# Inverse levels of a chunked scan: which half of the partitions holds a transposed inverse, and where the next head's keys are computed

## The chip, the cores and the metric

One NeuronCore of one Trainium2 chip runs the whole program. The time is device microseconds from launch to end; the median of the runs shown counts. PE is TensorE, PEld its weight loads, DVE VectorE, ACT ScalarE, POOL GpSimd, SP SyncE.

## The reference

Two layers of a hybrid trunk (an RWKV-7 mixer with a Fourier mixer, then a convolution mixer with gating), each followed by an expert-choice mixture of experts, for 512 sample tokens and 128 prompt tokens at width 1024. The change lies in the RWKV-7 mixer, 12 heads of 64 columns, both directions of time. Its recurrence, cut to what matters:

```python
def step(S, inp):
    r_t, w_t, k_t, v_t, kk_t, a_t = inp
    s_kk = jnp.einsum('zbhvk,zbhk->zbhv', S, kk_t)
    S = (S * w_t[..., None, :] - s_kk[..., None] * (kk_t * a_t)[..., None, :]
         + v_t[..., :, None] * k_t[..., None, :])
    return S, jnp.einsum('zbhvk,zbhk->zbhv', S, r_t)
```

All arithmetic is f32.

## The kernel before, in words

The recurrence is computed in tiles of 128 tokens. Within a tile the tokens' corrections of one another form a triangular system, and its 128x128 matrix has to be inverted, once for each of 5 tiles (the **groups** g below, NT = 5), 2 directions (z) and 2 heads (hh), since two heads make up the 128 partitions of one pass; there are six passes ("heads" in the code, `for i in range(HP - 1): heads(True)` and then `heads(False)`; "head" here means such a pass). The first five have `following` set: while one is scanned, the next one's projections are computed between its steps. The last one has no next.

A 128x128 triangle is treated as two 64x64 triangles and a corner. Each 64x64 triangle is inverted by doubling: in six **levels** blocks of 1, 2, 4, ... 32 are joined. `xx` holds, for each group, direction and head, the inverse (slot 1, `inv`) and its transpose (slot 0, `invT`) of both 64x64 blocks, one block in each half of the partitions. A block's inverse lies in the half in which the block itself lies in `mat`; its transpose lies in the other half. A level of one group goes round four engines' steps:

- `correct` (L1023), TensorE: 16 products of 64x64 from `yw` and `invT` into two PSUM banks, (4, 5) or (6, 7), by turns of the group's number. The first inner line (L1029) reads and writes the same half, the second (L1033) crosses to the other half. `first_correct` (L1011) does the same for the first level, where the products are mere copies and transposes.
- VectorE (L1646 to L1658): two predicated copies, one a direction, take the masked part of those banks into `xx` (`copy_predicated`, L1652); each of them says `x_new`.
- `middle` (L1036), TensorE: 8 products of 64x64 (L1043) of `mat`'s block and `inv`, all crossing, into bank 2 or 3.
- ScalarE (L1341 to L1344): one copy of 128x256 into `yw` says `yw_copied`.

The five groups run staggered, in an order written out by hand on TensorE (the listing below): first level; then a loop of four **turns**, each with the corrections of groups 0 to 4 and the middles of groups 3, 4, 0, 1, 2; then the last level, where `corner_middle` and `corner` make the corner blocks. A turn of the loop is a level of all five groups. `take(name, n)` waits for n signals.

Between the groups lie `keys` (L1064): matmuls of 128x128 by 128 columns that project one of the next head's five tiles of 128 tokens onto its keys, 8 for a tile, into PSUM banks 0 and 1. In the first level they stand in three places (3, 3 and 2 of the 8), in each turn in three places (2, 2 and 4).

VectorE does eight pieces of the previous head's output (`tail`, L1607: four reciprocals, scaling, shift, gate, bonus) in between, one after every third group from the start of the levels. After the last level, where it signals `x_new` only once its copies have ended (`done`), it copies the transposed inverses into `mat` (L1659 to L1661, ten copies), and TensorE waits for them (`blocks_copied`) and for the corners (`corner_copied`) before the scan (L1167).

TensorE's matrix is used in quarters here: with 64 rows read and 64 partitions written, four products can be in flight, each in its own quarter. An f32 product leaves two matmul records in the trace.

## Time and profile before

| | us |
|---|---|
| median of three runs | 2407.01 (2406.4 to 2408.57) |
| profiled execution, its own time | 2403.96 |
| its span, first to last instruction | 2402.1 |
| TensorE busy | 2259.6 (94%) |
| VectorE busy | 934.6 (39%) |
| ScalarE busy | 397.0 (17%) |
| mean granted TensorE clock | 0.982 of 2.4 GHz |

The busy time of TensorE is that of pipelined matmuls, so a busy TensorE need not be at its peak; shares over the whole span mix stages with different limits. The six heads lie between about 200 and 850 us of the span. The levels of head 0 run from 222.40 to 268.52, those of the last head from 798.67 to about 839.

### The profile page before, as it was taken

What the parts mean: (1) busy time and instruction counts of PE and PEld (TensorE: products, weight loads), DVE (VectorE), ACT (ScalarE), POOL (GpSimd) and SP (SyncE); (2) the same over time, 40 slices, a digit from 0 to 9 for tenths busy, and PEclk for the clock granted to TensorE, in tenths of its full rate; (3) what the DMA queues carried; (4) which work ended last, traced back from release to release, by engine and by line L of the source; (5) the groups of instructions that cost most, each with busy time, mean ns of one, the idle gap of its engine ahead of it and who ended that gap; (6) DMA issues with size and microseconds to landing.
All of it is one profiled execution on the core that took longest, in us unless ns stands there. A gap on an engine that the chain in (4) does not pass through costs nothing. (4 is left out here: it accounts for less than half of the span.)

```text
span 2402.1 us, 56100 instructions
## 1 busy us (share of the span) xinstructions
PE 2259.6 (94%) x23412; PEld 1292.7 (54%) x23412; DVE 934.6 (39%) x1965; ACT 397.0 (17%) x685; POOL 167.0 (7%) x162
## 2 busy tenths in 40 slices
PE   5998999999999889899999999889998999999997
PEld 2446777777686765544444444545555444444444
DVE  1357666676767621311111111479513111111113
ACT  2022323232323301100000000211312000000001
POOL 1001010100001000000000000000000000000000
PEclk8998999999999999999999999999999999999999
DMA  9981010101010025799999999602036999999995
GB/s 362 376 316 48 2 33 2 32 3 32 3 32 13 10 82 231 260 379 396 392 395 396 391 396 391 206 1 70 1 140 252 395 396 394 393 397 392 392 392 172
DMA packets 181670, 538.56 MB, mean 224 GB/s; under 512 B 12545, under 2 KB 54145, under 8 KB 181410
## 3 DMA queue, kind: packets, MB, share of 16 engines
q1 hardware_dynamic: 175202, 515.16, 55.8%
q0 software_dynamic: 6336, 21.63, 3.8%
q8 instruction: 84, 1.38, 0.2%
q14 instruction: 48, 0.39, 0.1%
HBM read 510.81 MB, written 25.95 MB: 223 GB/s over the span
## 5 line engine op out<-in xcount | busy, mean ns | idle before, releaser
L2115 PE MATMUL ps<-raw,xs 128*64 128x512 f32 x3072 | 670.9, 594 | 4.9 <-PEq L2109 4.9
L2115 PEld LDWEIGHTS ps<-raw,xs 128*64 128x64 f32 x3072 | 217.2, 137 | 429.4 <-issue 428.1
L2127 PE MATMUL ps<-raw,xs 128*32 128x256 f32 x6144 | 342.4, 380 | 2.2 <-PEq L2109 2.2
L2127 PEld LDWEIGHTS ps<-raw,xs 128*32 128x32 f32 x6144 | 195.2, 110 | 133.0 <-issue 9.7
L2306 DVE SCALAR_TENSOR_TENSOR h<-h,ps 128x768 f32<-128x768 f32 x32 | 30.5, 954 | 460.9 <-DVEq L2305 460.9
L1652 DVE COPY_PREDICATED wk<-m,ps 128x128 f32<-128x128 uint8 x360 | 101.8, 352 | 123.1 <-DVEq L1648 122.7
L2433 PE MATMUL ps<-h,raw 128*128 128x512 f32 (+1 forms) x448 | 124.0, 438 | 7.2 <-PEq L2424 7.2
L2234 ACT ACTIVATE h<-ps 128x768 f32<-128x768 f32 x32 | 25.9, 811 | 591.1 <-ACTq L2233 591.1
L899 PE MATMUL ps<-h,wk 128*128 128x512 f32 (+1 forms) x416 | 121.4, 438 | 1.5 <-PEq L1224 1.3
L1029 PE MATMUL ps<-wk 64*64 64x64 f32 x2400 | 102.2, 223 | 5.5 <-PEq L1005 5.2
L2433 PEld LDWEIGHTS ps<-h,raw 128*128 128x128 f32 x448 | 68.7, 193 | 62.0 <-issue 62.0
L1043 PE MATMUL ps<-wk 64*64 64x64 f32 x2400 | 97.0, 218 | 1.0 <-PEq L1005 0.8
L1033 PE MATMUL ps<-wk 64*64 64x64 f32 x2160 | 97.8, 222 | 0.1
L2694 DVE SCALAR_TENSOR_TENSOR wk<-wk 128x670 f32<-128x670 f32 x116 | 96.4, 914 | 0.4 <-DVEq L2688 0.4
L1344 ACT ACTIVATE wk<-ps 128x256 f32<-128x256 f32 (+1 forms) x180 | 65.8, 366 | 184.1 <-ACTq L1343 184.0
L2090 POOL DMA_INDIRECT ysum<-rows,idx x30 | 43.1, 1437 | 753.7 <-POOLq L2088 744.7
L899 PEld LDWEIGHTS ps<-h,wk 128*128 128x128 f32 x416 | 66.2, 191 | 53.5 <-issue 53.5
L1029 PEld LDWEIGHTS ps<-wk 64*64 64x64 f32 x2400 | 82.8, 133 | 14.2 <-issue 6.9
L1043 PEld LDWEIGHTS ps<-wk 64*64 64x64 f32 x2400 | 85.3, 135 | 1.6 <-issue 1.6
L2295 DVE TENSOR_TENSOR xs<-ps,mod 128x512 f32<-128x512 f32 x68 | 30.2, 486 | 140.3 <-DVEq L2292 140.3
L1641 DVE TENSOR_TENSOR wk<-ps,tables 128x512 f32<-128x512 f32 x120 | 74.6, 684 | 15.4 <-DVEq L1640 15.4
L1033 PEld LDWEIGHTS ps<-wk 64*64 64x64 f32 x2160 | 80.1, 134 | 0.2 <-issue 0.2
(333 smaller groups left out, 2673.5 us busy)
## 6 DMA issues: line engine op xcount, KB each, us to landing
raw<-in_moe_w_gate SPq DMA_DIRECT2D x64, 2048.0 KB, 17.5
raw<-in_moe_w_up SPq DMA_DIRECT2D x64, 2048.0 KB, 18.0
raw<-in_moe_w_down SPq DMA_DIRECT2D x64, 2048.0 KB, 18.3
wk<-in_mod_w SPq DMA_DIRECT2D x24, 2048.0 KB, 11.0
wk<-in_ev_w_in SPq DMA_DIRECT2D x18, 512.0 KB, 5.3
raw<-in_od_w_in SPq DMA_DIRECT2D x4, 2048.0 KB, 17.7
hrow<-rows SPq DMA_DIRECT2D x10, 512.0 KB, 3.0
ysum<-low SPq DMA_DIRECT2D x10, 512.0 KB, 8.9
```

The source lines that it names most:

```text
L899: last = pe.matmul(pair(q)[:, a:b], win[:, c, s], h[:, c, a:b], start=c == 0, stop=c == KC - 1)
L1029: pe.matmul(ps[lo:hi, zb, slotT(z, hh):slotT(z, hh) + HD], yw[lo:hi, g, z, hh], invT(g, z, hh, lo, hi), start=True, stop=True)
L1033: last = pe.matmul(ps[to:te, zb + 1, slotN(z, hh):slotN(z, hh) + HD], invT(g, z, hh, lo, hi), yw[lo:hi, g, z, hh], start=True, stop=True)
L1043: last = pe.matmul(ps[to:te, mbank(g), at:at + HD], mat[lo:hi, g, z, hh, 0, lo:hi], inv(g, z, hh, lo, hi), start=True, stop=True)
L1344: act.activation(yw[:, g].rearrange("p z h n -> p (z h n)")[:, 0:w], ps[:, mbank(g), 0:w], ACT.Copy).then_inc(sem("yw_copied"), 1)
L1641: dve.tensor_tensor(mat[:, tt, z, hh].rearrange("p k n -> p (k n)"), ps[:, 4 + (n + 2) % 4], tri[:, z], ALU.mult).then_inc(sem("mat_read"), 1)
L1652: dve.copy_predicated(changed(xx[:, g, z].rearrange("p k h n -> p k (h n)"), z, lev), changed(bcast(lv[:, lev, z], 1, 2), z, lev), changed ...
L2090: pool.indirect_dma_start(t["ysum"][:, :], bass.IndirectOffsetOnAxis(idx[:, e:e + 1], 0), ys[:, ee], None, compute_op=ALU.add).then_inc(se ...
L2115: last = pe.matmul(ps[to:to + CAPS, bank_of(kind, ee)], XS[ee][:, c, 0:CAPS], raw[:, slot(l, 2 * m + c // 4), c % 4, 8 * to:8 * to + 512], ...
L2127: last = pe.matmul(ps[to:to + 32, bank_of(kind, ee) + 1, 0:256], XS[ee][:, c, CAPS:], raw[:, slot(l, 2 * m + c // 4), c % 4, 8 * to:8 * to ...
L2433: last = pe.matmul(place(q)[:, a:b], win[m // 4][:, c, m % 4 * P:(m % 4 + 1) * P], h[:, c, a:b], start=c == 0, stop=c == KC - 1)
L2694: dve.scalar_tensor_tensor(to, src, cw[:, c, k:k + 1], to, ALU.mult, ALU.add).then_inc(sem("tap"), 1)
```

## The change

One of the four combinations of direction and head, (0, 0), keeps its transposed inverse in the half of its own block. For it, `correct`'s second product and `middle`'s product no longer cross; the product of `middle` goes to a place of its own in bank 1, the same one for all groups, so `middle` waits for its last copy. `correct` does the four combinations in another order, (0, 0) last. ScalarE copies a middle in two pieces (64 and 192 columns), each with a signal. VectorE copies a group in three pieces instead of two (four in the first level, with a wait), each with a signal. In the last level it copies the near transposed inverse over to the other half, where `corner` reads it from `yw`. The block copies into `mat` become six, each over all groups. All eight keys of a tile stand in one place: in the first level ahead of group 2's first correction, in a turn at its end. The tail pieces follow a level's fifth group: two behind each of the first three levels, then one and one. In the diff's core, `corrections` and `correction` are VectorE's copies:

```diff
+            TAIL = ((0, 1), (2, 3), (4, 5), (6,), (7,), ())
...
                         def correct(g, both=True):
...
+                            for z, hh in ((0, 1), (1, 0), (1, 1), (0, 0)):
+                                near = z == 0 and hh == 0
+                                for lo, hi in HALF:
+                                    pe.matmul(ps[lo:hi, zb, slotT(z, hh):slotT(z, hh) + HD], yw[lo:hi, g, z, hh], invT(g, z, hh, lo, hi), start=True, stop=True)
+                                for k, (lo, hi) in enumerate(HALF):
+                                    to, te = HALF[1 - k]
+                                    if near and (both or k == z):
+                                        last = pe.matmul(ps[lo:hi, zb, 4 * HD:5 * HD], invT(g, z, hh, lo, hi), yw[lo:hi, g, z, hh], start=True, stop=True)
+                                    if not near and (both or k != z):
+                                        pe.matmul(ps[to:te, zb + 1, slotN(z, hh):slotN(z, hh) + HD], invT(g, z, hh, lo, hi), yw[lo:hi, g, z, hh], start=True, stop=True)
                             last.then_inc(sem("z_ready"), 1)
...
+                        def middle(g, far_free, near_free):
+
+                            if far_free:
+                                take("yw_copied", far_free)
+                            for z, hh in ((0, 1), (1, 0), (1, 1)):
+                                for k, (lo, hi) in enumerate(HALF):
+                                    to, te = HALF[1 - k]
+                                    at = (z * 2 + hh) * HD
+                                    pe.matmul(ps[to:te, mbank(g), at:at + HD], mat[lo:hi, g, z, hh, 0, lo:hi], inv(g, z, hh, lo, hi), start=True, stop=True)
+                            if near_free:
+                                take("yw_copied", near_free)
+                            for lo, hi in HALF:
+                                last = pe.matmul(ps[lo:hi, 1, P:P + HD], mat[lo:hi, g, 0, 0, 0, lo:hi], inv(g, 0, 0, lo, hi), start=True, stop=True)
                             last.then_inc(sem("yw_ready"), 1)
...
                         with pe.Fori(0, LEVELS - 2) as lev:
+                            take("x_new", 6)
                             correct(0)
+                            middle(3, 1, 1)
                             correct(1)
+                            middle(4, 1, 1)
+                            take("x_new", 3)
+                            correct(2)
+                            middle(0, 3, 0)
+                            take("x_new", 3)
+                            correct(3)
+                            middle(1, 0, 1)
+                            take("x_new", 3)
+                            correct(4)
+                            middle(2, 1, 1)
                             if following:
+                                keys(lev)
...
+                            if u < NZ - NT:
+                                act.activation(product[:, 0:HD], ps[:, 1, P:P + HD], ACT.Copy).then_inc(sem("yw_copied"), 1)
+                                act.activation(product[:, HD:4 * HD], ps[:, mbank(g), HD:4 * HD], ACT.Copy).then_inc(sem("yw_copied"), 1)
...
+                            if lev == 0:
+                                correction(g, lev, 0, 0, 1, ps[:, zbank(g) + 1, 4 * HD:5 * HD]).then_inc(dve_done, 1)
+                                correction(g, lev, 0, 1, 2, ps[:, zbank(g), HD:2 * HD]).then_inc(new, 1)
+                                correction(g, lev, 0, 2, 4, ps[:, zbank(g) + 1, 0:2 * HD]).then_inc(new, 1)
+                                done()
+                                corrections(g, lev, 1).then_inc(new, 1)
+                            else:
+                                corrections(g, lev, 0).then_inc(new, 1)
+                                correction(g, lev, 1, 0, 3, ps[:, zbank(g), 2 * HD:5 * HD]).then_inc(new, 1)
+                                correction(g, lev, 1, 3, 4, ps[:, zbank(g) + 1, 3 * HD:4 * HD]).then_inc(new, 1)
                             if q >= NZ - NT:
-                                done(2)
-                                dve.sem_inc(sem("x_new"), 2)
-                            if q % 3 == 2 and q < 3 * KC:
-                                tail(q // 3, i)
+                                done(3)
+                                dve.tensor_copy(yw[0:HD, g, 1, 0], xx[HD:P, g, 0, 0, 0]).then_inc(dve_done, 1)
+                                done()
+                                dve.sem_inc(sem("x_new"), 3)
+                            if g == NT - 1:
+                                for k in TAIL[lev]:
+                                    tail(k, i)
                         for lo, hi in ((0, HD), (HD, P)):
-                            for g in range(NT):
-                                dve.tensor_copy(mat[lo:hi, g, :, :, 0, lo:hi], xx[P - hi:P - lo, g, :, 0]).then_inc(dve_done, 1)
-                        done(2 * NT)
+                            dve.tensor_copy(mat[lo:hi, :, 0, 0, 0, lo:hi], xx[lo:hi, :, 0, 0, 0]).then_inc(dve_done, 1)
+                            dve.tensor_copy(mat[lo:hi, :, 0, 1, 0, lo:hi], xx[P - hi:P - lo, :, 0, 0, 1]).then_inc(dve_done, 1)
+                            dve.tensor_copy(mat[lo:hi, :, 1, :, 0, lo:hi], xx[P - hi:P - lo, :, 1, 0]).then_inc(dve_done, 1)
+                        done(6)
```

## Rows read from the trace of the kernel before

In a windows row the stretch and its length come first, then busy us and instruction counts of PE, PEld, DVE, ACT and POOL.

**Rows 1.** Page, the 40 equal slices: busy tenths of the 16 DMA engines.
```profile
DMA  9981010101010025799999999602036999999995
```

**Rows 2.** Windows of head 0 by stage, then granted clock, DMA share, GB/s.
```profile
222.40:229.86 7.46, 6.75 (x165) 6.02 (x165) 4.41 (x11) 1.75 (x4) 0.00 (x0) 1.00 0.01 2
229.86:237.43 7.57, 7.57 (x257) 7.01 (x257) 5.50 (x12) 1.92 (x5) 0.00 (x0) 1.00 0.02 4
...
244.94:252.45 7.51, 7.51 (x257) 6.95 (x256) 3.74 (x12) 1.92 (x5) 0.00 (x0) 1.00 0.00 0
...
259.97:268.52 8.55, 7.69 (x241) 6.61 (x241) 5.09 (x24) 4.42 (x13) 1.56 (x3) 1.00 0.01 3
```

**Rows 3.** The same view, the four turns of the last head.
```profile
804.75:830.15 25.40, 20.81 (x963) 19.83 (x964) 17.17 (x49) 7.66 (x20) 0.00 (x0) 1.00 0.01 2
```

**Rows 4.** Timeline of TensorE in a turn: start us, us, line, tiles, count.
```profile
245.05 0.23 PE L1029 MATMUL ps<-wk 64*64 64x64 f32 x2
...
245.40 0.23 PE L1029 MATMUL ps<-wk 64*64 64x64 f32 x2
...
245.47 0.46 PE L1043 MATMUL ps<-wk 64*64 64x64 f32 x10
245.72 0.27 PE L1029 MATMUL ps<-wk 64*64 64x64 f32 x2
```

**Rows 5.** Timeline of TensorE around two key places of that turn.
```profile
243.85 1.16 PE L1068 MATMUL ps<-h,wk 128*128 x8
244.94 0.27 PE L1029 MATMUL ps<-wk 64*64 64x64 f32 x2
...
246.97 0.71 PE L1068 MATMUL ps<-h,wk 128*128 x4
247.61 0.27 PE L1029 MATMUL ps<-wk 64*64 64x64 f32 x2
```

**Rows 6.** Timeline of VectorE, head 0: a small instruction, copies, tail pieces.
```profile
204.78 0.26 DVE L1626 TENSOR_SCALAR wk<-wk 64x64 f32<-64x64 f32 x1
...
223.36 1.29 DVE L1652 COPY_PREDICATED wk<-m,ps 128x128 f32<-128x128 uint8 x4 [4.33 <-DVEq L1648]
...
231.26 1.11 DVE L1579 RECIPROCAL x<-x 128x160 f32<-128x160 f32 x1
...
245.82 0.49 DVE L1652 COPY_PREDICATED wk<-m,ps 128x128 f32<-128x128 uint8 x2 [0.96 <-DVEq L1648]
...
248.89 0.61 DVE L1589 TENSOR_SCALAR x<-x,wk 128x640 f32<-128x640 f32 x1
...
250.72 0.92 DVE L1652 COPY_PREDICATED wk<-m,ps 128x128 f32<-128x128 uint8 x4 [0.26 <-DVEq L1648]
```

**Rows 7.** Timeline of VectorE, head 0: last level, block copies, a dependent instruction.
```profile
260.82 0.50 DVE L1652 COPY_PREDICATED wk<-m,ps 128x128 f32<-128x128 uint8 x2 [1.67 <-DVEq L1648]
...
264.36 0.50 DVE L1652 COPY_PREDICATED wk<-m,ps 128x128 f32<-128x128 uint8 x2 [0.35 <-DVEq L1648]
265.10 2.24 DVE L1661 COPY wk<-wk 64x256 f32<-64x256 f32 x10 [0.24 <-DVEq L1454]
...
269.43 0.88 DVE L1491 SCALAR_TENSOR_TENSOR x<-x,wk 128x640 f32<-128x640 f32 x1 [0.16 <-DVEq L1454]
```

**Rows 8.** Timeline of ScalarE, head 0: copies of 256 and 128 columns.
```profile
246.24 0.38 ACT L1344 ACTIVATE wk<-ps 128x256 f32<-128x256 f32 x1 [1.80 <-ACTq L1343]
...
263.24 0.28 ACT L1344 ACTIVATE wk<-ps 128x128 f32<-128x128 f32 x1 [0.35 <-ACTq L1343]
```

**Rows 9.** Timelines of VectorE and TensorE, last head, end of first level.
```profile
803.32 1.29 DVE L1652 COPY_PREDICATED wk<-m,ps 128x128 f32<-128x128 uint8 x4 [0.26 <-DVEq L1648]
...
804.75 0.27 PE L1029 MATMUL ps<-wk 64*64 64x64 f32 x2 [1.35 <-PEq L1005]
```

**Rows 10.** Timeline of TensorE, head 0: fifth group's corner product, and the scan's start.
```profile
265.31 0.45 PE L1051 MATMUL ps<-wk 64*64 64x64 f32 x8
...
268.52 0.74 PE L1167 MATMUL ps<-wk 128*128 128x64 f32 x5 [0.48 <-PEq L1156]
```

More of the change, by code:

```diff
@@ L1025, in correct @@
                             zb = zbank(g)
-                            for z in range(2):
-                                for hh in range(2):
-                                    for lo, hi in HALF:
-                                        pe.matmul(ps[lo:hi, zb, slotT(z, hh):slotT(z, hh) + HD], yw[lo:hi, g, z, hh], invT(g, z, hh, lo, hi), start=True, stop=True)
-                                    for k, (lo, hi) in enumerate(HALF):
-                                        if both or k != z:
-                                            to, te = HALF[1 - k]
-                                            last = pe.matmul(ps[to:te, zb + 1, slotN(z, hh):slotN(z, hh) + HD], invT(g, z, hh, lo, hi), yw[lo:hi, g, z, hh], start=True, stop=True)
@@ L1034, in correct @@
-                            last.then_inc(sem("z_ready"), 1)
-                        def middle(g):
-                            for z in range(2):
-                                for hh in range(2):
-                                    for k, (lo, hi) in enumerate(HALF):
-                                        to, te = HALF[1 - k]
-                                        at = (z * 2 + hh) * HD
-                                        last = pe.matmul(ps[to:te, mbank(g), at:at + HD], mat[lo:hi, g, z, hh, 0, lo:hi], inv(g, z, hh, lo, hi), start=True, stop=True)
+                            for z, hh in ((0, 1), (1, 0), (1, 1), (0, 0)):
[8 more added lines that the diff above has]
+                                        pe.matmul(ps[to:te, zb + 1, slotN(z, hh):slotN(z, hh) + HD], invT(g, z, hh, lo, hi), yw[lo:hi, g, z, hh], start=True, stop=True)
@@ L1059, in corner, with keys @@
                                     at = (g - first) * P + hh * HD
-                                    last = pe.matmul(ps[lo:hi, bank, at:at + HD], yw[lo:hi, g, 0, hh], invT(g, z, hh, lo, hi), start=True, stop=True)
+                                    block = yw[lo:hi, g, 1, 0] if z == 0 and hh == 0 else invT(g, z, hh, lo, hi)
+                                    last = pe.matmul(ps[lo:hi, bank, at:at + HD], yw[lo:hi, g, 0, hh], block, start=True, stop=True)
                             if g == end - 1:
                                 last.then_inc(sem("corner_ready"), 1)
-                        def keys(tt, chunks):
+                        def keys(tt):
                             at = slice(tt * P, tt * P + P) if isinstance(tt, int) else bass.ds(tt * P, P)
-                            for c in chunks:
+                            for c in range(KC):
                                 last = pe.matmul(pair(0)[:, at], win[:, c, K], h[:, c, at], start=c == 0, stop=c == KC - 1)
-                            if chunks[-1] == KC - 1:
-                                last.then_inc(sem("keys_ready"), 1)
+                            last.then_inc(sem("keys_ready"), 1)
                         first_correct(0)
@@ L1080, in heads @@
                             take_weights()
-                            keys(ST, (0, 1, 2))
-                        take("x_new", 2)
+                            keys(ST)
+                        take("x_new", 3)
+                        first_correct(2)
+                        middle(0, 0, 0)
+                        take("x_new", 3)
                         first_correct(3)
-                        middle(1)
-                        if following:
-                            keys(ST, (3, 4, 5))
```

75 lines of the change are left out of this document (28 added, 47 removed).

## The prediction

> **What bounds the kernel now.** I read the page's slices first. From the middle on, the 16 DMA engines are busy nine tenths of the time with the experts' weights; in the slices of the even layer's heads (about 200 to 850 us) they are nearly idle [rows 1]. Nothing there waits for memory, and the experts' loads start when that layer ends, so a microsecond won or lost in a head should arrive at the end. The change touches one stretch of each of the six heads, the inverse levels. The stage windows cut head 0 by its turns: 7.46 us for the first level, about 7.5 for each of the four turns of the loop (two shown), 8.55 for the last level and the corners; TensorE is busy through every turn, at full clock (1.00, 2.4 GHz), VectorE for half to three quarters, ScalarE for a quarter [rows 2]. So the turns hang on TensorE. The last head has no next head whose keys it could compute: its turns take 25.40 us together, or 6.35 each, and TensorE has gaps [rows 3]. It shows what the turns wait for once the keys are gone.
>
> Inside a turn the array works in quarters: half of the rows read, half of the partitions written. A matmul leaves two records, and a quarter starts one every 0.059 us (six steps from 245.05 to 245.40, a seventh to the middle's first at 245.47 [rows 4]). Of a group's 24 products 8 stay in their own half and 16 cross, so each straight quarter has 8 records and each crossing quarter 16: 16 x 0.059 = 0.94 us a group, 4.72 for five. The keys make up the rest of 7.51: 2.8 us, though 16 records alone are 1.8: eight hold TensorE from 243.85 to 244.94, four from 246.97 to 247.61 [rows 5], so a record is (1.09 - 0.64) / 4 = 0.1125 us and a place costs (2.8 - 1.8) / 3 = 0.33 besides; 16 records in one place are 2.13.
>
> **What is taken away.** Two of three key places go: 0.67 us a turn. One product in four now stays straight, so each quarter gets 12 records: 12 x 0.059 = 0.71 us a group in place of 0.94. That needs straight records of the next part to run beside crossing ones of the part before. [Rows 4] show it: at 245.72 L1029 starts while six of the sixteen L1043 that stand ahead of it in the program are still to come. The near products share one place in PSUM, so each waits for ScalarE's copy of the one before: 0.06 (its second record), 0.36 (L1043's eighth start at 245.88 to ScalarE's at 246.24 [rows 4, 8]), 0.23 (the copy: 256 columns are 0.38, 128 are 0.28 [rows 8]) and 0.14 for the way back (804.61 to 804.75 [rows 9]): 0.79 us. Behind that wait in TensorE's queue stands the next correction. I take 0.71 a group where it does not bind and 0.78 where it does.
>
> **What is added.** VectorE's two copies a group become three (four, with a wait, in the first level). The columns stay the same; an instruction is added. From the third level on, two copies are 0.49 and four 0.92, so one every 0.21 [rows 6]: 0.13 for 128 columns and 0.08 besides; three then take 0.58. In the first two levels (four in 1.29, [rows 6]) the columns cost double: three 0.74, the first level's four 0.88. ScalarE copies twice a group; the far copy ends 0.46 after the near one starts, against 0.38. The tail pieces of the previous head's output, until now one after every third group, come in pairs after a level's fifth group: 1.11 and a pause, 2.64 a pair; the scale-and-shift pair, with 1.83 from its shift to the next copy, is 2.8 [rows 6]. In the last level each group gets a copy of 64 columns between two waits. Nothing is loaded, and no DMA queue moves.
>
> **The turn worked out**, from its first correction. The group's ten straight records bring VectorE's first copy at 0.95 (today 0.88 with eight: 244.94 to 245.82 [rows 5, 6]). With 0.58 and 0.14, the third correction may start at 1.67; TensorE would be there at 1.42. Group 4's near product starts last at 1.36, its far copy ends at 1.36 + 0.36 + 0.46 = 2.18, and the first group's middle, which today has keys ahead of it, starts at 2.32 and not at 2.08. The fourth correction follows at 2.62, the fifth at 3.40, the keys at 4.18, their end (2.13) at 6.3: against 7.51, 1.2 us won. Turn by turn:
> - First level: 1.2 for two groups, keys 2.13, then group 2 waits 0.95 + 0.88 + 0.14 for its copies, and so does group 4: 7.3 against 7.46. The keys' gain is lost because nothing now covers the last wait; the last head shows that wait open today, 1.35 us [rows 9].
> - Turn 1: the tail pair, begun when group 4's copies end 0.14 before the turn, holds VectorE until 2.50, the third correction waits until 3.38, the fifth for slow copies until 5.21; with 0.78 and 2.13, 8.1 against 7.57.
> - Turns 2 and 3: the pair runs 1.4 us into the turn, the third correction comes at 2.13, which costs 0.2: 6.55 each. Turn 4: 6.3.
>
> The turns make 27.5 against 30.1: 2.6 won, with the first level 2.8.
>
> **The last level** gives most of it back. There the groups follow one another on VectorE: copies begin at 260.82 and, four groups on, at 264.36, with a pause of 0.35 behind each group's wait [rows 7]. To each come 0.08 (third copy), a wait for the own result (0.16 at 269.43 [rows 7]) and a 64-column copy: a copy of 128 alone is 0.28 (0.49 - 0.21), half its columns less 0.22, and a 64x64 instruction is 0.26 [rows 6]; I take 0.22, by the price of the columns. That is 0.46 a group, 2.3 for five, less 0.15 where VectorE now waits for TensorE: 2.1 us. Behind the added waits stand the next group's copies, and TensorE's corrections and corner products wait for their release. The end cannot hide it: the fifth group's corner product (265.31 [rows 10]) waits for exactly this release. Bounds: 1.0, if copy and pause overlap; 2.6, if all of it counts. The block copies become six in place of ten, some 0.3 shorter; today they end at 267.34 [rows 7], and TensorE goes on at 268.52 [rows 10], so I count nothing.
>
> **Sum.** A head with keys: -2.8 + 2.1 = -0.7, five of them -3.4. The last head has no keys to merge: turn 1 at 7.0, then 6.4 and 6.55 with tail pairs uncovered, and 5.1, 25.1 against 25.40 [rows 3]; with 2.1 from the last level, +1.8. Together -1.6 us. The profiled execution took 2403.96 us, 3.05 below the median of the runs; it would take 2402.4, and the median 2407.01 becomes **2405.5**.
>
> **The rivals.**
> - *Slower: the quarters don't mix (0.12).* If straight records wait until the crossing ones ahead of them have started, a group's parts line up: ten records, then six, then the near pair, 1.0 us where today's is 0.94. Turns 2 to 4 stay near 7.5, turn 1 takes 8.5, the last level's 2.1 is left: +3 a head, +18 in all, 2425. With the step at 0.85 it would be some +5, 2412; from there the change loses. [Rows 4] speak against it. The Trainium skill (TensorE: Matmul & The Clock Gate, Part 3, What overlaps and what doesn't) says that matmuls are strictly first in, first out in start and end; by that rule this rival would be the forecast, and the start at 245.72 contradicts it here.
> - *Slower: a predicated copy has one price whatever its width (0.12).* No row shows one of 96 or 32 columns. At 0.21 (0.28 early) each, VectorE takes 0.71 a group and 1.01 early, the first level's chain grows by 0.8, turn 1 by 0.6, turns 2 and 3 by 0.4 each, the last level by 0.7: +2.9 a head over the forecast, +15, 2421; at half of it 2413. It decides from about 0.65 a group. The other instructions of [rows 6] get shorter with width, which speaks against it.
> - *Faster: the last level costs only its lower bound (0.30).* If the added copy starts inside the pause that is there anyway, the price is 1.0, a head wins 1.8, the last loses 0.7: -8, 2399. For it: a group's 0.35 already holds one wait. Against it: the copy reads what the three before it wrote, so its own wait must come first.
> - *The forecast (0.46)*, 2402 to 2411: gain in the turns and price in the last level cancel.
>
> A measurement of this kernel tells about 0.2%, 4.8 us, from no change. Faster by more is the third rival, 0.30; slower by more the first two, 0.24; between them 0.46. The range runs from 2397 (the third rival with a turn a little better than worked out) to 2414 (half of either slower rival).
>
> **What would show it.** In the changed profile: one key place a turn of 16 records in about 2.1 us; L1029's successor and the middle starting within each other, 0.71 to 0.78 us between corrections; turns of 8.1, 6.55, 6.55 and 6.3; in turn 1 an idle TensorE for 1.5 us or more while VectorE does two reciprocals in a row; in the last level VectorE's groups 1.3 us apart in place of 0.85, and the corners about 2 us later. Wrong would be: groups 0.9 us or more apart (first rival), copies of 32 columns as long as those of 128 (second), last-level groups under 1.1 us apart (third).

## The result, and the profile after

The changed kernel takes 2417.78 us (median of five runs, 2416.72 to 2418.23); the kernel before took 2406.40 beside it. The ratio is 1.0048, 95% interval 1.0036 to 1.0059: **slower by 11.4 us**, outside the forecast range. The profiled execution took 2418.23 us with a span of 2416.3, that of before 2403.96 with 2402.1.

Where the 14.2 us between the two spans lie follows from two moments of each head, its first correction and the start of its scan, read from TensorE's timeline:

| us | before | after |
|---|---|---|
| levels of heads 0 to 5 | 46.10, 46.56, 46.51, 46.27, 46.38, 40.19 | 46.01, 49.83, 49.11, 47.83, 47.67, 41.71 |
| their sum | 272.0 | 282.2 |
| between the heads' levels | 344.4 | 344.7 |
| behind the last head's levels | 1563.2 | 1568.0 |
| ahead of the first | 222.4 | 221.5 |

The levels lose 10.1 us, and all of it in heads 1 to 4 and the last; head 0, by which the forecast was worked out, gains 0.1. The part behind the levels grows by 4.8. The change does not touch it, and it lies anywhere between 1563 and 1572 us in the fourteen kernels profiled here, one execution each, with the kernel before at the low end; what moves it is not shown.

The windows of after, by stage, columns as in [rows 2]: head 0's first level, turns 1, 2 and 4 and last level; turn 1 of heads 1 to 4; the last head's four turns.

```profile
221.46:228.62 7.16, 6.16 (x185) 5.75 (x185) 3.95 (x21) 1.93 (x7) 0.00 (x0) 1.00 0.01 2
228.62:236.54 7.92, 6.56 (x257) 6.18 (x257) 6.48 (x19) 2.22 (x10) 0.00 (x0) 1.00 0.02 4
236.54:243.27 6.73, 6.59 (x257) 6.29 (x257) 4.97 (x18) 2.23 (x10) 0.00 (x0) 1.00 0.00 0
250.00:256.73 6.73, 6.63 (x257) 6.34 (x256) 3.59 (x17) 2.23 (x10) 0.00 (x0) 1.00 0.00 0
256.73:267.47 10.74, 8.39 (x241) 7.04 (x241) 6.65 (x29) 4.49 (x14) 1.56 (x3) 1.00 0.01 2
344.05:355.67 11.62, 8.30 (x256) 7.68 (x257) 7.50 (x19) 2.22 (x10) 0.00 (x0) 0.86 0.01 3
463.07:472.89 9.82, 7.01 (x256) 6.39 (x256) 6.55 (x19) 2.23 (x10) 0.00 (x0) 1.00 0.01 3
580.60:590.34 9.74, 7.08 (x257) 6.54 (x257) 7.51 (x19) 2.23 (x10) 0.00 (x0) 1.00 0.03 6
697.06:706.63 9.57, 6.84 (x257) 6.35 (x257) 7.52 (x19) 2.23 (x10) 0.00 (x0) 1.00 0.01 3
812.36:837.65 25.29, 18.45 (x960) 17.47 (x961) 18.70 (x69) 8.90 (x40) 0.00 (x0) 1.00 0.01 2
```

Against [rows 2], head 0 wins 0.30 in the first level, loses 0.35 in turn 1, wins 0.78 in each later turn and loses 2.19 in the last level. Turn 1 is the same program in every head, yet takes 7.92, 11.62, 9.82, 9.74 and 9.57; turns 2 to 4 of heads 0 to 4 are 6.73 to 6.84. The kernel before had a trace of this already, which the prediction did not look at: turn 1 of heads 1 to 4 took 8.02, 7.99, 7.73 and 7.72 against head 0's 7.57. Two of them, and an idle time in the first that waits for nothing ("issue"), 0.24 us before a middle:

```profile
344.98:353.00 8.02, 7.78 (x256) 7.12 (x256) 5.49 (x12) 1.92 (x5) 0.00 (x0) 1.00 0.01 3
690.73:698.45 7.72, 7.72 (x256) 7.16 (x257) 5.49 (x12) 1.92 (x5) 0.00 (x0) 1.00 0.01 2
...
351.54 0.45 PE L1043 MATMUL ps<-wk 64*64 64x64 f32 x8 [0.24 <-issue]
```

TensorE's timeline of after, turn 1 of head 1:

```profile
347.25 0.27 PE L1032 MATMUL ps<-wk 64*64 64x64 f32 x2 [1.36 <-PEq L1006]
...
349.08 0.33 PE L1032 MATMUL ps<-wk 64*64 64x64 f32 x4
351.37 0.27 PE L1038 MATMUL ps<-wk 64*64 64x64 f32 x2 [1.96 <-issue]
...
352.22 3.52 PE L1079 MATMUL ps<-h,wk 128*128 x16
```

The 1.36 is the forecast's wait for VectorE's two reciprocals. The 1.96 is new: TensorE **stops** in the middle of group 4's correction: it is idle and waits for nothing that the profile shows ("issue"). Then the 16 key records take 3.52 us in place of 2.05, at a granted clock of 0.54 from 352.22 to 355.67, nearly all of it at the lower level of 1.2 GHz; it was 1.00 from 351.37 to 352.22. Heads 2, 3 and 4 stop for 0.76 and 1.63, for 1.31 and for 1.30 at other lines; head 0 does not stop.

What comes at those moments stands in the DMA view. The page of after has two queues of instructions, and does not say whose. One of them, q8, is read here as that of TensorE's program, because each stop follows one of its packets; it has 85 packets in 1.39 MB over the span (packets, MB, share of 16 engines):

```profile
q8 instruction: 85, 1.39, 0.2%
```

The DMA view of after, cut to 348.90 to 349.90:

```profile
q8 instruction: 1, 0.02, 5.8%
```

From 344.05 to 348.90, the first 4.85 us of this turn, there is no packet; one starts at 348.96 and ends at 349.88, and 1.49 us later TensorE goes on. Laid beside each other, with the place in TensorE's program as the fraction of a block of 256 instructions (counted from the program's start: four instructions a product, since the trace has two PE and two PEld records for each; two a transposition, one a wait):

```
after    stop   goes on at  packet           end to go on  place
head 1   1.96   351.37      348.96 to 349.88  1.49         0.77
head 2   0.76   465.38      462.79 to 464.06  1.32         0.77
head 2   1.63   470.25      467.60 to 468.81  1.44         0.78
head 2   1.28   501.53      498.94 to 500.25  1.29         (corners)
head 3   1.31   587.87      585.47 to 586.62  1.25         0.78
head 4   1.30   704.65      702.27 to 703.33  1.32         0.79
```

What tells here is that the fraction is nearly the same each time; why its value is 0.77 and not 1 is left open.

So **theory A**: in the first pass through the loop TensorE reaches the end of a block of its program before the next block has come. The Trainium skill (Runtime: NRT & Kernel Launch, Instruction fetch mechanics) says that an engine's program comes in blocks of 16 KiB, 256 instructions, by a DMA queue of the sequencer's own, the next while the present one runs, and that the cost of crossing is mostly hidden. The trace agrees with the blocks (1.39 MB in 85 packets is 16.4 KB each) and not with the last point here. The idle 0.24 us of the kernel before end 1.26 us behind a packet's end as well (350.28). Turns 2 to 4 of head 0 show no packet and no stop: their code is there by then. **Theory B**: the stops belong to heads 1 to 4 for a reason of their own, such as the previous head's pieces.

### The profile page after: what moved, and what is told of

Read it like the earlier page. It is cut to its first block and busy times, and to the rows that moved or that the text cites. A ratio compares the mean times of both kernels' runs of the same rounds, so it can differ in the third digit from the quotient of the medians.

```text
span 2416.3 us, 56886 instructions
## 1 busy us (share of the span) xinstructions
PE 2249.0 (93%) x23532; PEld 1283.9 (53%) x23532; DVE 953.7 (39%) x2181; ACT 406.6 (17%) x835; POOL 167.8 (7%) x162
## 3 DMA queue, kind: packets, MB, share of 16 engines
q8 instruction: 85, 1.39, 0.2%
## 5 line engine op out<-in xcount | busy, mean ns | idle before, releaser
L2148 PEld LDWEIGHTS ps<-raw,xs 128*32 128x32 f32 x6144 | 195.2, 110 | 133.8 <-issue 10.4
L1032 PE MATMUL ps<-wk 64*64 64x64 f32 x2400 | 100.6, 221 | 27.0 <-PEq L1006 25.1
L1032 PEld LDWEIGHTS ps<-wk 64*64 64x64 f32 x2400 | 84.7, 134 | 32.9 <-issue 30.2
L1636 DVE COPY_PREDICATED wk<-m,ps 128x128 f32<-128x128 uint8 x180 | 62.5, 347 | 68.8 <-DVEq L1658 67.8
L1049 PE MATMUL ps<-wk 64*64 64x64 f32 x1800 | 84.1, 224 | 2.9 <-issue 2.1
L1642 DVE COPY_PREDICATED wk<-m,ps 128x32 f32<-128x32 uint8 (+2 forms) x390 | 71.6, 247 | 38.1 <-DVEq L1658 37.9
L1038 PE MATMUL ps<-wk 64*64 64x64 f32 x1620 | 80.8, 225 | 2.0 <-issue 2.0
L979 PE MATMUL ps<-wk 64*128 64x256 f32 x480 | 68.0, 406 | 12.7 <-PEq L973 6.6
L2334 DVE COPY xs<-ps 128x256 f32<-128x256 f32 x32 | 13.6, 425 | 145.4 <-DVEq L2333 145.4
```

The costliest lines, as they stand in the source:

```text
L979: last = pe.matmul(ps[:, 4 + (n + 2 + hh) % 4, k * 256:(k + 1) * 256], src[lo:hi, z, tt], ar[lo:hi, z, tt], start=True, stop=True)
L1032: pe.matmul(ps[lo:hi, zb, slotT(z, hh):slotT(z, hh) + HD], yw[lo:hi, g, z, hh], invT(g, z, hh, lo, hi), start=True, stop=True)
L1038: pe.matmul(ps[to:te, zb + 1, slotN(z, hh):slotN(z, hh) + HD], invT(g, z, hh, lo, hi), yw[lo:hi, g, z, hh], start=True, stop=True)
L1049: pe.matmul(ps[to:te, mbank(g), at:at + HD], mat[lo:hi, g, z, hh, 0, lo:hi], inv(g, z, hh, lo, hi), start=True, stop=True)
L1636: return dve.copy_predicated(changed(xx[:, g, z].rearrange("p k h n -> p k (h n)"), z, lev), changed(bcast(lv[:, lev, z], 1, 2), z, lev), ...
L1642: return dve.copy_predicated(changed(out, z, lev), changed(bcast(lv[:, lev, z, 0:HD], 1, b - a), z, lev), changed(src.rearrange("p (k n) - ...
```

## The experiments

A **place** below is how many instructions into the loop a block ends, counted so that the stops of after stand at ends of blocks; one stop can so stand at the place and another 256 instructions behind it, still in the loop's 532. For heads 0 to 4 it is 121, 150, 179, 208 and 237 in the changed kernel (43 in the last head): 29 more each time, since a head has 2275 instructions, 29 fewer than nine blocks. All are read like the table above; "levels" is the sum over the six heads in the one profiled execution, whose own time can lie off the median: 2404.15 us in pad25, 2407.18 in early_tail, 2402.09 in keys_one.

| run | median us | ratio to before, 95% | levels |
|---|---|---|---|
| before / after | 2406.40 / 2417.78 | 1.0048 [1.0036, 1.0059] | 272.0 / 282.2 |
| pad25 | 2411.68 | 1.0025 [1.0012, 1.0038] | 276.6 |
| pad54 | 2418.58 | 1.0050 [1.0034, 1.0067] | 281.8 |
| tail_spread | 2424.13 | 1.0066 [1.0045, 1.0086] | 288.1 |
| defer_copy | 2413.32 | 1.0030 [1.0018, 1.0041] | 279.8 |
| keys_three | 2416.03 | 1.0049 [1.0032, 1.0066] | 285.4 |
| keys_one | 2405.96 | 1.0005 [0.9994, 1.0016] | 271.2 |
| aligned_defer | 2407.16 | 1.0008 [0.9998, 1.0018] | 267.0 |
| aligned_early | 2402.59 | 0.9989 [0.9979, 0.9998] | 265.6 |
| early_tail | 2403.14 | 0.9991 [0.9983, 1.0000] | 276.3 |
| keys_first | 2405.26 | 0.9992 [0.9981, 1.0003] | 270.9 |
| aligned_waits | 2405.43 | 0.9998 [0.9989, 1.0007] | 269.4 |
| aligned_short | 2404.44 | 0.9990 [0.9981, 0.9999] | 268.9 |

**Moving the program (pad25, pad54).** One line; nothing in the levels is touched.

```diff
                     mod_turn(pe, PARTS - EARLY, 5)
+                    keep_busy(pe, 4, 25)    # pad54: 54
                     for i in range(HP - 1):
```

> The changed kernel with 25 more matmuls of 128x128 by 128 columns on TensorE ahead of the first head, where TensorE waits for some 5 us anyway. They add work that nothing reads, and move the program of TensorE by 100 instructions. Theory A (TensorE stops in turn 1 of heads 1 to 4 because the next 256 instructions of its program have not come yet): the stops stand where a block of 256 ends, so they move with the program. By the count of instructions a block then ends 21, 50, 79, 108 and 137 instructions into the loop of heads 0 to 4, in place of 121, 150, 179, 208 and 237; the one head without a stop had 121. Turn 1 of heads 0 to 3 should take 7.9 to 8.3 us and have no stop over 0.8 us that waits for nothing, head 4 is open; about 7 us are won, some 2411 us. Theory B (the stops belong to heads 1 to 4 for a reason of their own, such as the previous head's pieces on VectorE or ScalarE): turn 1 stays at 9.6 to 11.7 us in heads 1 to 4, the stops stand before the same lines, and the time stays at 2418 us.

> The same with 54 matmuls: the program moves by 216 instructions, and a block of 256 ends 161, 190, 219, 248 and 21 instructions into the loop of heads 0 to 4. Theory A: now heads 0, 1 and 2 stop in turn 1 for 1.2 us or more each, head 0 among them, which had no stop, and head 4 stops no more (turn 1 about 8 us there); head 3 is open. The time is 2416 to 2420 us. Theory B: head 0 stays without a stop at 7.9 us, heads 1 to 4 keep theirs.

Turn 1 in pad25, heads 0, 1, 4 and the last:

```profile
224.28:232.48 8.20, 6.63 (x256) 6.26 (x257) 6.78 (x19) 2.23 (x10) 0.00 (x0) 1.00 0.02 4
339.58:347.50 7.92, 6.57 (x257) 6.17 (x257) 6.50 (x19) 2.23 (x10) 0.00 (x0) 1.00 0.02 4
...
683.43:691.34 7.91, 6.56 (x256) 6.18 (x257) 6.48 (x19) 2.23 (x10) 0.00 (x0) 1.00 0.02 4
797.52:805.93 8.41, 5.36 (x240) 4.78 (x241) 5.54 (x18) 2.16 (x10) 0.00 (x0) 1.00 0.01 2
```

Heads 1 to 4 all take 7.91 and their levels 46.02, as head 0 does in after. The last head, whose place moved from 43 to 199, now loses: 46.04 against 41.71. TensorE's timeline in pad54, turn 1 of heads 0, 1 and 2:

```profile
234.16 0.37 PE L1036 MATMUL ps<-wk 64*64 64x64 f32 x2 [1.94 <-issue]
...
350.96 0.21 PE L1049 MATMUL ps<-wk 64*64 64x64 f32 x1 [0.91 <-issue]
...
355.96 0.27 PE L1032 MATMUL ps<-wk 64*64 64x64 f32 x3 [1.98 <-issue]
...
474.92 0.33 PE L1049 MATMUL ps<-wk 64*64 64x64 f32 x4 [1.32 <-issue]
```

Head 0, at place 161, now stops for 1.94 and takes 10.06; head 3 stops for 0.64, head 4 (place 21) no longer. The stops moved with the program, as theory A said, and theory B falls. Over the changed kernel and the twelve experiments there are 50 stops of over 0.6 us in the levels that wait for nothing: every one ends 1.20 to 1.56 us after a packet's end, and the 48 whose place can be read lie at 0.765 to 0.796 of a block. pad25's runs spread from 2404 to 2419 us, and the profiled one is the fastest; the median holds something that this trace does not show. The program behind the heads moves too.

**What holds the fetch back (tail_spread).** VectorE's pieces as before the change; TensorE's program is the same.

```diff
-                            if g == NT - 1:
-                                for k in TAIL[lev]:
-                                    tail(k, i)
+                            if q % 3 == 2 and q < 3 * KC:
+                                tail(q // 3, i)
```

> The changed kernel with the pieces of the previous head's output on VectorE one after every third group, as before the change, in place of two after a level's fifth group. TensorE's program is the same instruction by instruction. If the long wait of TensorE early in turn 1 (1.3 us for the pair) is what holds back the fetch of its next instructions, the stops of 1.3 us and more in turn 1 shrink or go, turn 1 comes to 7.5 to 8.5 us in all heads and the time to some 2409 us. If the burst of products behind the wait alone outruns the fetch, stops of over 1 us stay in heads 1 to 4 and the time is 2414 to 2418 us. If the pair costs nothing but its own wait, turn 1 of head 0 gains 0.5 to 1.0 us and turns 2 and 3 lose as much.

Turn 1 of heads 1 and 4 (the last three columns: granted clock, DMA share, GB/s):

```profile
345.42:353.23 7.81, 7.81 (x256) 7.62 (x256) 5.44 (x17) 2.23 (x10) 0.00 (x0) 0.78 0.02 4
696.05:707.63 11.58, 9.33 (x257) 8.72 (x257) 5.56 (x17) 2.23 (x10) 0.00 (x0) 0.71 0.02 4
```

Heads 1 and 2 have no stop of over 0.6 us any more (turn 1 at 7.81 and 8.28), heads 3 and 4 still do, head 4 for 1.73 and 0.53. So the long wait is not the only cause, and where it falls changes who stops. The first level grows from 7.16 to 7.88 us, turn 2 from 6.73 to 7.12, the last head's levels from 41.71 to 44.73, and the time is worse than either time that the readings gave. Part of it is the clock: granted over turn 1 were 0.78, 0.78, 0.79, 0.82 and 0.71 in heads 0 to 4, where after has 1.00 in all but head 1. So this run compares two things at once, and does not say how much the pieces alone cost. In after, the packet of head 0's turn 1 starts at 230.28, ahead of its wait's end at 231.82; in head 1, with the block's end 29 instructions later in the loop, it starts at 348.96, 1.7 us behind the wait's end at 347.25. That the request stands in the program behind that wait fits, but is argued and not shown.

**The parts of the change (keys_one, keys_three).** keys_one is the kernel before with each tile's eight keys in one place (the turn's part of the edit; the first level's is alike):

```diff
                             middle(4)
-                            if following:
-                                keys(lev, (0, 1))
...
                             middle(1)
-                            if following:
-                                keys(lev, (2, 3))
...
                             if following:
-                                keys(lev, (4, 5, 6, 7))
+                                keys(lev)
```

keys_three is pad25 with the turns' keys in three:

```diff
                             middle(4, 1, 1)
+                            keys(lev, (0, 1))
...
                             middle(1, 0, 1)
+                            keys(lev, (2, 3))
...
                             middle(2, 1, 1)
-                            keys(lev)
+                            keys(lev, (4, 5, 6, 7))
```

> The kernel before with one part of the change alone: all eight keys of a tile in one place, ahead of group 2 in the first level and at the end of a turn. Forecast's step: each turn loses two places, 0.67 us, so turns 2 to 4 come to 6.85 us in place of 7.51. Rival (quarters bind a turn and the places cost less): 7.2 us or more. The last level stays at 4.7 us a head. Theory A adds that stops which wait for nothing may stand in turn 1 here too, since TensorE goes through a turn's instructions faster between the keys; the place where a block ends is 163, 240, 61, 138, 215 and 69 instructions into the loop, as in the kernel before.

> The changed kernel with the 25 idle matmuls ahead of the first head (the run in which turn 1 had no stops in heads 1 to 4), and with the keys of a turn in three places as before the change (2, 2 and 4 of the 8); those of the first level stay in one place. Forecast's step (a place costs 0.33 us): turns 2 to 4 come to 7.2 to 7.4 us in place of 6.73. Rival (the places cost nothing, since keys cover waits for VectorE): turns 2 to 4 stay at 6.7 to 6.8 us, and turn 1 falls under 7.6 us because its wait of 1.35 us is covered.

Turns 2 and 3 of head 0 in keys_one:

```profile
236.34:243.64 7.30, 7.10 (x257) 6.81 (x256) 4.22 (x12) 1.92 (x5) 0.00 (x0) 1.00 0.00 0
243.64:250.86 7.22, 7.02 (x257) 6.72 (x256) 3.71 (x12) 1.92 (x5) 0.00 (x0) 1.00 0.00 0
```

Turns 3 and 4 of head 1 in keys_three:

```profile
358.83:366.18 7.35, 6.90 (x257) 6.29 (x256) 4.84 (x19) 2.22 (x10) 0.00 (x0) 1.00 0.00 0
366.18:373.01 6.83, 6.83 (x257) 6.27 (x256) 3.50 (x17) 2.23 (x10) 0.00 (x0) 1.00 0.00 1
```

Two key places fewer a turn are worth 0.2 to 0.3 us a turn alone, not 0.67: the rival held. With the near product they are worth 0.1 to 0.6 (6.83 and 7.35 to 6.73); of keys_three's two readings neither held whole, since turns 2 and 3 (7.30 and 7.35) come out as the forecast's step says and turn 4 (6.83) nearly as the rival does. keys_one also stops in turn 1: head 1, place 240, by 0.77 us and head 4, place 215, by 1.68 (9.55). keys_three does in heads 3 and 4, the second time by 2.24:

```profile
699.75 0.21 PE L1049 MATMUL ps<-wk 64*64 64x64 f32 x1 [2.24 <-issue]
```

So either half of the change exposes the fetch. And the place alone does not decide: head 4 has place 137 in keys_three and in pad25, and in pad25 it does not stop. The place says where TensorE can stop; what else decides whether it does, such as when the packet was asked for, is not shown. The last level is 8.56 in keys_one, as in [rows 2]: its price belongs to the near half.

**The last level (defer_copy).**

```diff
                                 done(3)
-                                dve.tensor_copy(yw[0:HD, g, 1, 0], xx[HD:P, g, 0, 0, 0]).then_inc(dve_done, 1)
-                                done()
-                                dve.sem_inc(sem("x_new"), 3)
+                                dve.sem_inc(sem("x_new"), 2)
+                                dve.tensor_copy(yw[0:HD, g, 1, 0], xx[HD:P, g, 0, 0, 0]).then_inc(sem("x_new"), 1)
```

> The changed kernel, but in the last level VectorE tells TensorE that a group's three copies have ended before it makes the 64-column copy, and that copy has a signal of its own, which only the corner product reads for. Forecast's step (the copy and the wait behind it cost 0.16 + 0.22 us a group): groups on VectorE come about 0.9 to 1.0 us apart in place of 1.24, and the last level falls by 1.2 to 1.9 us a head, so 7 to 11 us over the six heads, to about 2409 us. Rival (the last level hangs on something else, such as TensorE's own products or the corner copies): it stays at about 6.9 us a head and the time within 3 us of 2418.

VectorE's timeline in after, first two groups of head 0's last level, and the block copies' first and last:

```profile
257.67 0.30 DVE L1636 COPY_PREDICATED wk<-m,ps 128x128 f32<-128x128 uint8 x1 [1.55 <-DVEq L1658]
257.88 0.35 DVE L1642 COPY_PREDICATED wk<-m,ps 128x96 f32<-128x96 uint8 x2
258.37 0.19 DVE L1673 COPY wk<-wk 64x64 f32<-64x64 f32 x1
258.91 0.30 DVE L1636 COPY_PREDICATED wk<-m,ps 128x128 f32<-128x128 uint8 x1 [0.35 <-DVEq L1658]
...
264.05 0.35 DVE L1680 COPY wk<-wk 64x320 f32<-64x320 f32 x1 [0.24 <-DVEq L1453]
...
265.95 0.54 DVE L1682 COPY wk<-wk 64x640 f32<-64x640 f32 x1
```

The same of defer_copy:

```profile
256.03 0.30 DVE L1637 COPY_PREDICATED wk<-m,ps 128x128 f32<-128x128 uint8 x1 [1.54 <-DVEq L1659]
256.23 0.35 DVE L1643 COPY_PREDICATED wk<-m,ps 128x96 f32<-128x96 uint8 x2
256.82 0.19 DVE L1675 COPY wk<-wk 64x64 f32<-64x64 f32 x1 [0.24 <-DVEq L1454]
257.05 0.30 DVE L1637 COPY_PREDICATED wk<-m,ps 128x128 f32<-128x128 uint8 x1
```

The first two groups come 1.24 apart in after and 1.02 in defer_copy, against a mean of 0.89 over the four steps of [rows 7]; a head's last level falls from 10.74 to 9.86, 0.88 us, less than the 1.2 to 1.9 expected: the copy itself stays on VectorE's path, only the waits around it go. Its median is 4.5 us under that of after, though it stops in four heads (head 2, at place 177, takes 12.93 in turn 1, at a granted clock of 0.60).

**Keeping the place (aligned_defer).** defer_copy, with the place at 85 in heads 0 to 4.

```diff
                     def heads(following):

+                        keep_busy(pe, 6, 7 if following else 12)
```

> The changed kernel with the deferred 64-column copy, and with 7 idle matmuls at the start of each head (2 more ahead of the first, 12 in the last), which nothing reads. They keep the place at which a block of 256 instructions ends the same in every head: 85 instructions into the loop, 98 in the last head; the heads without a stop had 50 to 137. Theory A (stops are set by that place): no stop over 0.8 us in turn 1 of any head, turn 1 at 7.9 us in heads 0 to 4 and 6.9 to 7.2 us in the last, the levels at 45.1 us a head from first correction to scan, five times, and 41.4 us in the last. Together 267 us against 272.0 us before: about 2401 us. Rival (the stops only seemed to follow the place): some heads stop again and the time is 2408 us or more. Rival (the idle matmuls lie on the path): the rest of a head grows by 0.8 us from 68.9 us, and the time is about 2405 us.

Turn 1 takes 7.92, 7.91, 7.91, 7.90, 8.11, and 7.19 in the last head; the levels are 45.12 or 45.13 in four heads, 45.31 and 41.18: theory A to 0.2 us. The levels win 5.0 us, but the time is that of before, not 2401: the parts between the heads grow by 3.1 together, so the idle matmuls are partly on the path (the second rival), and the part behind the heads, 1563.2 before, is 1570.3 in this trace.

**One reciprocal earlier (aligned_early, early_tail, keys_first).** All three are defer_copy with the first reciprocal in VectorE's pause of the first level. aligned_early keeps place 85; early_tail has pad25's line in its stead, so places 21 to 133, and 20 idle matmuls in the last head's first level; keys_first is early_tail with a turn's keys moved from its end to its start.

```diff
-            TAIL = ((0, 1), (2, 3), (4, 5), (6,), (7,), ())
+            TAIL = {1: (0,), 4: (1,), 9: (2, 3), 14: (4, 5), 19: (6,), 24: (7,)}
...
-                            if g == NT - 1:
-                                for k in TAIL[lev]:
-                                    tail(k, i)
+                            for k in TAIL.get(q, ()):
+                                tail(k, i)
```

> The same, with the first of the eight pieces (a reciprocal of 1.1 us) behind the second group of the first level, where VectorE waits 1.8 us for TensorE's keys, so that one reciprocal and not two stands between the first level and turn 1. Theory V (VectorE's pair sets turn 1): the wait of TensorE for 1.35 us in turn 1 falls to 0.3 us or less, turn 1 comes to 6.8 to 7.1 us, 4 to 5 us are won over six heads, about 2396 us. Theory F (a block of instructions takes about 4 us to come, and the first pass through the loop needs two): turn 1 stays at 7.5 to 8 us or more, with a stop that waits for nothing in place of the wait for VectorE, and the time within 2 us of the run above.

> The deferred 64-column copy and the first reciprocal behind the second group of the first level, as in the run before, but the program is moved by 25 idle matmuls ahead of the first head alone, so that heads 0 to 4 have a block's end 21, 49, 77, 105 and 133 instructions into the loop and pay for no idle matmuls; the last head has 20 of them in its own waits of the first level (114 instructions). Theory F (a block takes about 4 us to come, and the first pass through the loop needs two): turn 1 stays between 7.4 and 8.1 us at all these places, the levels near 44.7 to 45.3 us a head. Theory V (VectorE's pair set turn 1, and 85 instructions was a bad place): turn 1 is under 7.2 us in at least two heads. With the idle matmuls off the path the rest of a head falls from 69.9 to 68.9 us. Time about 2399 us, 2396 to 2403.

> The same, with the keys of a turn at its start in place of its end. They then stand in TensorE's wait of 0.9 us behind the first level, and take 2.05 us for 65 instructions of the program, in which a block can come; the last level starts without keys ahead of it. Theory F: turn 1's stops go, its groups follow at 0.75 to 0.85 us, and the levels fall by 0.5 to 1.5 us a head against the run above, to 43.3 to 44.5 us. Rival: the wait opens again ahead of the last level (0.9 us there), and the levels stay within 0.3 us of the run above.

Turn 1 in aligned_early, heads 0, 1 and 3:

```profile
226.91:234.69 7.78, 6.81 (x257) 6.38 (x257) 5.57 (x18) 2.23 (x10) 0.00 (x0) 1.00 0.02 4
342.19:350.24 8.05, 6.81 (x256) 6.38 (x256) 5.62 (x18) 2.23 (x10) 0.00 (x0) 1.00 0.02 4
...
570.89:578.36 7.47, 6.83 (x257) 6.41 (x257) 5.55 (x18) 2.23 (x10) 0.00 (x0) 1.00 0.02 5
```

The wait for VectorE is gone, and in all five heads a stop of 0.6 to 1.2 us has taken its place, as theory F said: turn 1 hardly falls. The time fell by 4.6 us against aligned_defer, though, where theory F had it within 2; the levels win only 1.4 of that, and what won the rest is not shown. In early_tail turn 1 takes 8.44, 7.60, 7.79, 8.25 and 10.66 (places 21 to 133): neither theory's range held, and place 133 stops by 2.18 us where pad25's 137 did not. Its last head's levels take 47.23, but about 2.5 us of that are the idle matmuls, which did not fit into the waits: its first level, from the first correction to turn 1, takes 9.03 us, and 6.50 in aligned_early, which has none there.

```profile
792.15:801.18 9.03, 8.96 (x209) 8.48 (x209) 5.82 (x22) 1.93 (x7) 0.00 (x0) 1.00 0.01 3
```

keys_first gave 8.66, 7.38, 7.08, 7.87 and 7.66, but its later turns are 7.00 to 7.44, and the levels of heads 1 to 3 are those of early_tail to 0.2 us: there its rival held.

**Idle matmuls inside a wait (aligned_waits, aligned_short).** As aligned_early, place 61, with 7 idle matmuls in the wait behind the first level; in aligned_short they have 16 columns.

```diff
-                        keep_busy(pe, 0, 7)
+                        for _ in range(7):
+                            pe.matmul(ps[:, 0, 0:16], ident, ident[:, 0:16], start=True, stop=True)
```

> The deferred 64-column copy and the early reciprocal, with a block's end at the same place in every head as in the second run before, but 61 instructions into the loop (70 in the last head), and the idle matmuls where TensorE waits anyway: 8 ahead of the first head, 7 in each head's wait of 0.9 us behind the first level, 6 in place of the last head's missing keys. Theory A (the place sets the stops): turn 1 is within 7.4 to 8.1 us in all of heads 0 to 4, no head has 8.5 us or more as the run with 21 to 133 instructions had in two, the last head's levels come to 41.2 us and not 47.2; the levels make 265 to 267 us against 272.0 before. With the rest of a head at 68.9 to 69.2 us the time is about 2400 us, 2398 to 2404. Rival (the spread of turn 1 has little to do with the place): some head takes 8.5 us or more, and the time is 2403 us or more.

> The run before with the 7 idle matmuls behind the first level cut to 16 columns each. Of 128 columns they were 14 records of 0.12 us, 1.6 us in a wait of 0.9 us, and the first level grew by 0.75 us. If that was all they cost, the first level comes back to 3.85 us from the first middle's copy to the fourth's, turn 1 stays between 7.0 and 8.0 us in heads 0 to 4 (place 61, as before), the levels make 264 to 267 us against 272.0 in the kernel before, and the time is 2400 to 2403 us. Rival (the idle matmuls gave the block the time to come, and turn 1 needs it): turn 1 grows by what the first level wins, and the levels stay near 269 us.

Turn 1 takes 7.91, 7.26, 7.64, 6.98, 7.40 and then 7.82, 7.11, 7.13, 7.73, 7.47, so theory F's floor of 7.4 is not one; no head reaches 8.5. The time of aligned_waits, 2405 us, is still that of its rival. The first level is 0.7 dearer in both, and the levels stay near 269: the narrow matmuls took as long as the wide ones, so aligned_short did not make room as it was meant to, and its question stays open. Their matmuls and their weight loads (PEld):

```profile
340.76 1.73 PE L1101 MATMUL ps<-cst 128*128 128x16 f32 x14
...
340.76 1.64 PEld L1101 LDWEIGHTS ps<-cst 128*128 128x128 f32 x14
```

The lowest median is that of aligned_early, 3.5 us under the 2406.05 of before beside it, with an interval that just excludes 1. So does that of aligned_short, and early_tail's ends at 1.0000; of twelve variants the best was picked, so a win over the kernel before is not firmly shown.

## Why the prediction was wrong

- **The failed step** is "Nothing is loaded, and no DMA queue moves", and with it "-0.7, five of them": head 0 stood for five heads. TensorE's program is itself loaded, by a queue in the page that was not read, and a faster turn 1 runs into it: that wait was put at nothing. Of the five heads the first happens to have a place without a stop. Against the 46.02 us of a head without stops, heads 1 to 4 lose 3.81 + 3.09 + 1.81 + 1.65 = 10.4 us, which is the loss. The stops make 7.5 us of it (the one of 0.76 is left out, since the wait for VectorE behind it shrinks from 1.35 to 0.43), head 1's keys at the lower clock 1.5; 1.4 us are not traced. No rival named it.
- **The rest of the sum**, taken without stops, is nearly right: five heads at 46.02 and the last at 41.71 make 271.8 against 272.0, so -0.2 where -1.6 was forecast. pad25 shows four more such heads, aligned_defer five with the deferred copy, at 45.1 to 45.3.
- *First level and turns*: forecast 7.3, 8.1, 6.55, 6.55, 6.3; head 0 took 7.16, 7.92, 6.73, 6.73, 6.73. In the later turns the mis-sized term is the start of the fourth and fifth corrections: VectorE's timeline of turn 4 (from 250.00), third to fifth group:

```profile
252.62 0.31 DVE L1636 COPY_PREDICATED wk<-m,ps 128x128 f32<-128x128 uint8 x1 [0.40 <-DVEq L1658]
...
253.82 0.30 DVE L1636 COPY_PREDICATED wk<-m,ps 128x128 f32<-128x128 uint8 x1 [0.64 <-DVEq L1658]
...
254.76 0.30 DVE L1636 COPY_PREDICATED wk<-m,ps 128x128 f32<-128x128 uint8 x1 [0.39 <-DVEq L1658]
```

  By the forecast (0.95 behind a correction's start) they stand at 2.62, 3.57 and 4.35: the third is exact, the fourth 0.25 and the fifth 0.41 late. ScalarE's far copy of group 4, for which group 0's middle waits, ends 2.42 us into the turn in place of 2.18, and its near copies follow at 0.83 us, not 0.78:

```profile
252.10 0.32 ACT L1341 ACTIVATE wk<-ps 128x192 f32<-128x192 f32 x1
253.29 0.22 ACT L1340 ACTIVATE wk<-ps 128x64 f32<-128x64 f32 x1 [0.87 <-ACTq L1338]
...
254.12 0.23 ACT L1340 ACTIVATE wk<-ps 128x64 f32<-128x64 f32 x1 [0.38 <-ACTq L1338]
```

- *A key place at 0.33*: wrong; keys_one shows 0.10 to 0.15. The two halves do not add up: in turn 4 the merged places win 0.29 alone and 0.10 behind the near product, the near product 0.68 alone and 0.49 behind them; in turn 3 it wins 0.16 alone.
- *The last level, +2.1*: 2.19 in head 0, with groups 1.24 apart (forecast 1.3). The 64-column copy took 0.19 (0.22), and 0.48 in the third group. Block copies: 2.44 us in six against 2.24 in ten [rows 7], where 0.3 less was expected.
- *The last head, +1.8*: +1.52, its turns 25.29 against 25.1 forecast.
- *The rivals*: the quarters mix: near products come 0.83 apart, just under the 0.85 from which that rival began, and the turns take 6.73, not 7.5. A copy of 96 and one of 32 columns take 0.35 together, less than two of 128 at 0.49, so width counts. The last level's lower bound of 1.0 did not come; even with the copy off the signal it costs 1.31.

## What to carry to other kernels

Read every repetition of an unrolled stage, not the first: five copies of one code that differ by tenths before a change, as turn 1 did here (7.57 to 8.02), point at something that the first copy does not show. Where a change makes an engine run through its program faster, look at the instruction queue in the DMA view, and at idle time that waits for nothing; in these runs the first pass of the loop and the straight code behind it pay for it, and turns 2 to 4 have no such stop. Before a change of a few microseconds is judged, move the program by some idle instructions: here that alone was worth 6 us. And take the trace of one execution for one execution: pad25's runs spread over 15 us.

## What was not expected of the hardware

- TensorE's program comes in 16 KB packets that take 0.9 to 1.6 us in the heads, and TensorE goes on 1.20 to 1.56 us after the packet's end when it had to wait; stops are up to 2.24 us long (keys_three, head 4).
- After such a stop the granted clock fell in head 1 of after: 1.00 until 352.22, then 0.54 over 3.45 us, which cost 1.5 us in the keys. Heads 2 to 4 stopped as well and kept 1.00; tail_spread has 0.78 in turn 1 of heads 0 and 1 without a stop. What sets it stays open.
- An f32 matmul of 128x128 by 16 columns takes as long as one by 128: 14 records in 1.73 us, 0.124 each, where the keys' 16 take 2.05. Their weight loads, of 128 columns each, follow one another all that time (14 in 1.64 us), so it looks as if the weights decide; no run here varies them alone. The Trainium skill (TensorE: Matmul & The Clock Gate, LDWEIGHTS) gives a load as its columns over 1.2 in ns, by which 128 columns would be an estimated 107 ns; the trace agrees within a sixth.
